# One encoder kernel: every fourth wide tile takes its products in mirrored order

## The chip, the cores and the metric

The kernel runs on one core of one Trainium2 chip. The metric is the device time of one execution in microseconds (us). Before the change three runs took 1983.12, 1983.80 and 1987.77 us, so the median is 1983.8 us.

## The reference

Two layers over 256 tokens of width 1024. Each layer is a normalisation, a projection to attention, Hyena and gate inputs, the two mixers, an output projection, and then a PEER block. The PEER block is what the change touches:

```
q = h @ wq                                   # 1024 -> 2048, per token
s = q . subkeys ; top 16 x top 16 -> 16 experts of 16384 per head
a = gelu(h . u_tab[expert])                  # first expert product
y = sum over heads and experts of g * a * v_tab[expert]
```

The kernel computes `h @ u` for all 16384 experts (128 tiles of 128 experts), multiplies the result by a routing weight that is zero for the experts not picked, and multiplies by `v` (128 more tiles).

## The kernel before, in words

All weights come from memory as one stream of tiles of 128 x 1024 numbers into a ring of four places. Every tile is split into a high part (ScalarE, L507, rounded to the short format that TensorE multiplies at full rate) and a low part, the rest (GpSimd or VectorE, L444). The activations are split the same way. A product is then high by high, high by low and low by high.

Two forms of this product stand in the kernel. In the trunk (`contract`, `product`; lines 1611 to 1635) each of the three products is a matmul of its own with 256 moving columns, one for each token. In the query projection (16 tiles a layer) and the first expert product (128 tiles a layer) `wide_tile` is used: the moving operand of the high weights is the high and the low activations side by side, so one matmul with 512 columns (L1646, the wide product) does two of the three, and one with 256 columns (L1648, the narrow product) does the third with the low weights. Both are added up in one bank of PSUM over eight steps k. Every matmul has its own weight load of 128 x 128, so that a tile is eight wide and eight narrow products and sixteen loads, always in the order wide, narrow, wide, narrow. The second expert product (`v_half`, L2045) has 512 columns in all three of its products.

The order of TensorE's queue is written out by hand. `wide_tile` waits for the low part of a half tile (`parts_ready`) before steps 0 and 4. A tile's last matmul raises `tile_done`. Behind that ScalarE copies the bank's right half out (L825, L849), splits the tile two ahead (L507), and GpSimd makes its low part (L444), which the tile two ahead waits for. VectorE adds the two halves and ScalarE applies the gelu, which frees the bank (`gelu_done`).

The wide tiles of a layer are called from five places: four query tiles in a row and then a loop with four a turn; `u_tile` for the first 60 expert tiles, four written out and the rest in loops with four a turn; `late_tile` for the last 68, with four in each of 16 turns of a loop, each turn begun by 32 small matmuls of routing weights (L1984), and two ahead of and two behind that loop.

Of the kernel before, what the change touches and what calls it, by code (L numbers as in the profile page):

```python
# [22 lines left out]
S = 256  # L23
# [16 lines left out]
KT = D // P  # L40
# [5 lines left out]
T_UP, T_OUT, T_WQ, T_U = 40, 48, 56, 72  # L46
# [3 lines left out]
AHEAD = 2  # L50
SORTED = 52
ROUTED = 60
# [45 lines left out]
def encoder_kernel(nc, x_in, stream, subkeys, cols, ffn_cols, w1_in, w2_in, w3_in, skip_in, rpb_in,  # L98
                   pos_in, dft_in, decay_in, spread_in, mask_in, mats_in, iota_in, out):
    ctx = ExitStack()  # L100
    with ctx:
        def sb(name, shape, dt=F32):
            return ctx.enter_context(nc.sbuf_tensor(name, shape, dt))
# [14 lines left out]
        w_hi = sb("w_hi", [P, 2 * AHEAD, HT], F32R)  # L118
        w_lo = sb("w_lo", [P, 2 * AHEAD, HT], F32R)
# [19 lines left out]
        bank = [ctx.enter_context(nc.psum_tensor(f"bank{i}", [P, 512], F32)) for i in range(8)]  # L139
# [24 lines left out]
        both_raw = raw_parts2[:, :, :].rearrange("p (b k) t -> p b k t", b=2)  # L164
        both_acts = act_parts[:, :, :, :]
# [1430 lines left out]
        def _(pe):  # L1596
            T = nc.tensor

            def pe_layer(l):
                def parts_ready(i, tile, half):  # L1600

                    pe.wait_ge(lo_ready[half].sem, lo_ready[half].at(l, i * RING + (tile + 1)))

                def weights(part_, tile, k):

                    return part_[:, 2 * (tile % AHEAD) + k // 4, (k % 4) * P:(k % 4 + 1) * P]

                def product(out_, tile, j, k, start, stop, parts=(act_hi, act_lo)):

                    hi, lo = parts  # L1610
                    T.matmul(out_, weights(w_hi, tile, j), hi[:, k, :], start=start, stop=False,
                             skip_group_check=True)
                    T.matmul(out_, weights(w_hi, tile, j), lo[:, k, :], start=False, stop=False,
                             skip_group_check=True)
                    return T.matmul(out_, weights(w_lo, tile, j), hi[:, k, :], start=False, stop=stop,
                                    skip_group_check=True)
# [19 lines left out]
                                       skip_group_check=True)  # L1636
                    return ins

                def wide_tile(out_, i, tile, both, wait=None):

                    for k in range(KT):
                        if k % 4 == 0:
                            parts_ready(i, tile, k // 4)
                        if wait is not None:
                            wait(k)
                        T.matmul(out_[:, 0:2 * S], weights(w_hi, tile, k), both[:, :, k, :],  # L1646
                                 start=(k == 0), stop=False, skip_group_check=True)
                        ins = T.matmul(out_[:, 0:S], weights(w_lo, tile, k), both[:, 0, k, :],  # L1648
                                       start=False, stop=(k == KT - 1), skip_group_check=True)
                    ins.then_inc(tile_done.sem, 1)  # L1650

                def trunk_part(n):
# [23 lines left out]
                def head_columns(i):  # L1676
                    return by_head[:, QUAD - 2 - 2 * i:2 * QUAD - 2 - 2 * i]
# [59 lines left out]
                for e in range(TT):  # L1737
                    ins = T.matmul(bank[5][e * FFN:(e + 1) * FFN, 0:P], w1[0:POS, :], pos[0:POS, e, :],
                                   start=True, stop=True)
                ins.then_inc(ffn_done.sem, 1)  # L1740

                for n in range(4):
                    if n == 1:
                        pe.wait_ge(tile_copied.sem, tile_copied.at(l, 8))
                        for i in range(2):
                            for j in range(4):
                                ins = T.matmul(bank[4][j * QUAD:(j + 1) * QUAD, 0:S], head_columns(i),
                                               qk_sq[:, 2 * j + i, :], start=(i == 0), stop=(i == 1))
# [3 lines left out]
                    for half in range(2):  # L1752
                        parts_ready(0, T_V + n, half)
                        k, part_ = 2 * n + half, 2 * (n % AHEAD) + half
                        for tt in range(TT):
                            tokens = slice(tt * P, (tt + 1) * P)
                            T.matmul(bank[6 + tt][:, :], raw_hi[1][:, k, tokens], w_hi[:, part_, :],
                                     start=(k == 0), stop=False)
                            T.matmul(bank[6 + tt][:, :], raw_hi[1][:, k, tokens], w_lo[:, part_, :],
                                     start=False, stop=False)  # L1760
                            ins = T.matmul(bank[6 + tt][:, :], raw_lo[1][:, k, tokens], w_hi[:, part_, :],
                                           start=False, stop=(k == KT - 1))
                    ins.then_inc(tile_done.sem, 1)
                    if n == 3:
                        pe.wait_ge(arg_ready.sem, arg_ready.at(l, 1))
                        pe.wait_ge(sin_done.sem, sin_done.at(l, 1))
                        for e in range(TT):
                            rows = slice(e * FFN, (e + 1) * FFN)
                            ins = T.matmul(bank[5][rows, 0:P], w2[rows, :], h1[rows, :], start=True, stop=True)
# [24 lines left out]
                for n in range(4):  # L1794
# [3 lines left out]
                    ins = T.matmul(bank[4 + n][:, :], dft[:, ri, e, 0:P], filters[:, ri, e, :], start=True, stop=True)  # L1798
# [35 lines left out]
                for h in range(NH):  # L1834
# [4 lines left out]
                    for qt in range(TT):  # L1839
                        for kt in range(TT):  # L1840
                            ins = T.transpose(bank[6][:, kt * S + qt * P:kt * S + (qt + 1) * P],
                                              probs[:, h % 2, qt, kt * P:(kt + 1) * P], identity)
# [15 lines left out]
                    for kt in range(TT):  # L1858
                        for j in range(2):
                            g = h - 1 + j  # L1860
                            ins = T.matmul(attn_ps[h // 2][j * HD:(j + 1) * HD, :], v_tok[:, kt, g * HD:(g + 1) * HD],
                                           probs_T[:, j, kt, :], start=(kt == 0), stop=(kt == TT - 1))
# [26 lines left out]
                for ct in range(4):  # L1889
                    for e in range(TT):  # L1890
                        for ri in range(2):
                            ins = T.matmul(bank[4 + ct][:, e * P:(e + 1) * P],
                                           spec_y[:, ri, e, ct * P:(ct + 1) * P], dft[:, 2 + ri, e, 0:P],
                                           start=(ri == 0), stop=(ri == 1))
# [4 lines left out]
                for k in range(4):  # L1899
                    pe.wait_ge(hyena_ready.sem, hyena_ready.at(l, k + 1))  # L1900
                    for j in (0, 1):
                        ins = product(bank[(8 + j) % 4][:, 0:S], T_UP + 4, 4 * j + k, 4 + k, k == 0, k == 3)
# [6 lines left out]
                def out_product(m, k):  # L1909

                    if k % 4 == 0:
                        parts_ready(0, T_OUT + m, k // 4)
                    if m == 0:
                        pe.wait_ge(up_used.sem, up_used.at(l, 8 + k + 1))
                    return product(bank[4 + m % 4][:, 0:S], T_OUT + m, k, k % 4, k == 0, k == KT - 1,
                                   (act_hi, act_lo) if k < 4 else (merged_hi, merged_lo))
# [16 lines left out]
                for m in range(8):  # L1933
# [5 lines left out]
                    for k in range(2 if m == 1 else 0, KT):  # L1939
# [3 lines left out]
                        ins = out_product(m, k)  # L1943
                    ins.then_inc(tile_done.sem, 1)

                for s in range(RING):
                    if s == 1:
                        mean_square(2)
                    wide_tile(bank[s % 4], 0, T_WQ + s, both_raw, trunk_part(2) if s == 0 else None)
                with pe.Fori(1, (T_U - T_WQ) // RING) as w:  # L1950
                    for s in range(RING):
                        pe.wait_ge(q2_ready.sem, q2_ready.at(l, w * RING + (s - 3)))
                        wide_tile(bank[s % 4], w, T_WQ + s, both_raw)
                pe.wait_ge(subk_in.sem, subk_in.at(l, 16))
                for n in range(8):
                    tt, g = n // 4, n % 4
# [4 lines left out]
                    for c in range(4):  # L1961
                        m = 4 * g + c
                        ins = T.matmul(bank[4 + g][:, c * P:(c + 1) * P], q2T[:, m, tt * P:(tt + 1) * P],
                                       subk[:, m, :], start=True, stop=True)
                    ins.then_inc(score_done.sem, 1)

                def u_tile(i, s, first):


                    if first + s >= 4:  # L1970
                        pe.wait_ge(gelu_done.sem, gelu_done.at(l, i * RING + (first + s - 3)))
                    wide_tile(bank[s % 4], i, T_U + first + s, both_acts)

                def late_tile(i, n):

                    pe.wait_ge(gelu_done.sem, gelu_done.at(l, i * RING + (ROUTED + n - (3 if n < AHEAD else 1))))
                    wide_tile(bank[n % 2], i, T_U + ROUTED + n, both_acts)

                def routing_weights(i, n):

# [21 lines left out]
                for s in range(RING):  # L2002
                    u_tile(0, s, 0)
                with pe.Fori(0, SORTED // RING - 1) as i:
                    for s in range(RING):
                        u_tile(i, s, RING)
                pe.wait_ge(slots_ready.sem, slots_ready.at(l, 1))
                for tt in range(TT):
                    for c in range(3):
                        ins = T.transpose(bank[6 + tt][:, c * P:(c + 1) * P], slots[:, tt, c, :], identity)  # L2010
                    ins.then_inc(slotT_done.sem, 1)
                with pe.Fori(0, (ROUTED - SORTED) // RING) as i:
                    for s in range(RING):
                        u_tile(i, s, SORTED)

                for n in range(AHEAD):
                    late_tile(0, n)
                pe.wait_ge(gelu_done.sem, gelu_done.at(l, ROUTED))
                with pe.Fori(0, TGROUPS // RING) as i:
                    for n in range(BURST):  # L2020
                        routing_weights(i, n)
                    for n in range(BURST):
                        late_tile(i, n + AHEAD)
                for n in range(LATE - AHEAD, LATE):
                    late_tile(0, n)
# [69 lines left out]
            for l in range(DEPTH):  # L2095
                pe_layer(l)
# [113 lines left out]
```

## Time and profile before

| | |
|---|---|
| median of three runs | 1983.8 us |
| the profiled execution | 1983.6 us |
| its span, first to last instruction | 1981.8 us |
| TensorE matmuls | busy 1975.0 us, 100% of the span, 11924 instructions |
| TensorE weight loads | busy 1717.0 us, 87% |
| GpSimd, VectorE, ScalarE | busy 81%, 63%, 56% |
| granted TensorE clock | 1.000 (2.4 GHz) |

A matmul's record is longer than its share of the engine: matmuls are pipelined, and a record runs from its start to a modelled end, so that records overlap. What one product costs is therefore read from the distance between two starts, not from its mean duration.

### The profile page before, as it was taken

To read this page: it belongs to the slowest core of one execution; us is meant where nothing else is said; L and a number is where in the kernel's file an instruction comes from. 1 tells how busy PE (TensorE), PEld (TensorE's weight loads), DVE (VectorE), ACT (ScalarE), POOL (GpSimd) and SP (SyncE) were. 2 spreads that over 40 slices of the span, in tenths; PEclk is the share of its full clock that TensorE was granted. 3 is DMA by queue.
4 is the path that set the end of the run, shared out by engine and by line. 5 is a ranking of instruction groups with operands and counts; after the bars stand their busy time and mean duration, and the time that the engine had idled before them with its cause. 6 is when DMAs were issued, how large, how long until landed. Compare 5 with 4: busy or idle time off the path is not lost.

```text
span 1981.8 us, 41411 instructions
## 1 busy us (share of the span) xinstructions
PE 1975.0 (100%) x11924; PEld 1717.0 (87%) x11924; DVE 1246.6 (63%) x2807; ACT 1119.1 (56%) x2455; POOL 1603.1 (81%) x1316
## 2 busy tenths in 40 slices
PE   9999999999999999999999999999999999999999
PEld 8999888888888888888888898888888888888887
DVE  6787589888886333333367865998888863333333
ACT  6565565655555555555575556666555555555554
POOL 7767979987778888888877678899877878888886
PEclk9999999999999999999999999999999999999999
DMA  9544645554445555555584446455544455555554
GB/s 279 171 140 150 210 160 182 189 178 160 160 159 167 193 191 192 195 194 190 196 234 163 138 159 211 161 190 184 174 163 165 159 169 194 191 191 193 194 195 149
DMA packets 103396, 358.41 MB, mean 181 GB/s; under 512 B 11744, under 2 KB 16802, under 8 KB 103076
## 3 DMA queue, kind: packets, MB, share of 16 engines
q1 hardware_dynamic: 102900, 355.41, 54.5%
q10 hardware_dynamic: 432, 2.18, 0.3%
q8 instruction: 36, 0.59, 0.1%
q14 instruction: 28, 0.23, 0.0%
HBM read 356.49 MB, written 1.05 MB: 180 GB/s over the span
## 4 chain that ended last, share of the span: by engine, by line
PE 60%; POOL 23%; issue 15%; POOLq 1%; DMA 0%; DVE 0%; SPq 0%; ACT 0%; DVEq 0%; ACTq 0%
PE bank L2045 35%; POOL w_lo L444 23%; PE bank L1646 14%; PE bank L1648 7%; PE bank L1984 3%; POOLq L442 0%; DMA ring<-stream 0%; POOLq L465 0%; PE bank L2071 0%; POOL e_lo L472 0%; SPq L409 0%; SPq L413 0%; DVE raw_lo L974 0%; PE bank L2010 0%; ACT w_hi L507 0%
## 5 line engine op out<-in xcount | busy, mean ns | idle before, releaser
L444 POOL TENSOR_TENSOR w_lo<-ring,w_hi 128x512 fp32r<-128x512 f32 x1048 | 1400.9, 1353 | 289.5 <-ACT w_hi L507 288.3
L507 ACT ACTIVATE w_hi<-ring 128x512 fp32r<-128x512 f32 x1312 | 753.3, 621 | 186.7 <-PE bank L1635 88.1
L1646 PE MATMUL bank<-act_parts,w_hi 128*128 128x512 f32 x2048 | 718.1, 396 | 0.2
L1648 PE MATMUL bank<-act_parts,w_lo 128*128 128x256 f32 x2048 | 569.6, 278 | 0.0
L444 DVE TENSOR_TENSOR w_lo<-ring,w_hi 128x512 fp32r<-128x512 f32 x256 | 236.7, 924 | 450.1 <-ACT w_hi L507 449.9
L1646 PEld LDWEIGHTS bank<-act_parts,w_hi 128*128 128x128 f32 x2048 | 384.1, 188 | 89.6 <-POOL w_lo L444 1.3
L2045 PE MATMUL bank<-w_hi,e_hi 128*128 128x512 f32 x1024 | 398.9, 390 | 0.2
L2045 PE MATMUL bank<-w_hi,e_lo 128*128 128x512 f32 x1024 | 398.4, 389 | 0.0
L2045 PE MATMUL bank<-w_lo,e_hi 128*128 128x512 f32 x1024 | 398.4, 389 | 0.0
L1648 PEld LDWEIGHTS bank<-act_parts,w_lo 128*128 128x128 f32 x2048 | 385.2, 188 | 0.0
L843 ACT ACTIVATE e_hi<-arena 128x256 fp32r (+1 forms) x256 | 106.8, 418 | 315.6 <-PE bank L2045 315.6
L472 POOL TENSOR_TENSOR e_lo<-arena,e_hi 128x256 fp32r<-128x256 f32 x256 | 191.7, 749 | 70.7 <-ACT e_hi L843 70.6
L2045 PEld LDWEIGHTS bank<-w_hi,e_hi 128*128 128x128 f32 x1024 | 192.2, 188 | 41.4 <-POOL e_lo L472 1.0
L2045 PEld LDWEIGHTS bank<-w_hi,e_lo 128*128 128x128 f32 x1024 | 192.2, 188 | 39.9
L2045 PEld LDWEIGHTS bank<-w_lo,e_hi 128*128 128x128 f32 x1024 | 192.2, 188 | 39.4
L849 ACT ACTIVATE norm_tmp<-bank 128x256 f32<-128x256 f32 x136 | 52.6, 387 | 202.9 <-PE bank L1648 202.9
L1630 PE MATMUL bank<-act_parts,w_hi 128*128 128x256 f32 x896 | 121.3, 288 | 0.0
L1630 PEld LDWEIGHTS bank<-act_parts,w_hi 128*128 128x128 f32 x896 | 111.2, 191 | 9.4 <-issue 7.9
L825 ACT ACTIVATE arena<-bank 128x256 f32<-128x256 f32 x120 | 46.1, 384 | 125.9 <-PE bank L1648 125.9
L1541 DVE TENSOR_TENSOR bank<-bank,norm_tmp 128x256 f32<-128x256 f32 x136 | 58.6, 431 | 63.2 <-ACT norm_tmp L849 63.2
L1523 DVE TENSOR_TENSOR weighted_j<-onehot_j,bank 128x512 f16<-128x512 f16 x256 | 95.2, 413 | 0.0
L1646 PE MATMUL bank<-raw_parts,w_hi 128*128 128x512 f32 x256 | 89.4, 394 | 0.0
(262 smaller groups left out, 2357.6 us busy)
## 6 DMA issues: line engine op xcount, KB each, us to landing
ring<-stream SPq DMA_DIRECT2D x654, 512.0 KB, 3.3
arena<-rpb_in SPq DMA_DIRECT2D x8, 512.0 KB, 8.5
arena<-dft_in SPq DMA_DIRECT2D x4, 512.0 KB, 5.8
arena<-subkeys ACTq DMA_DIRECT2D x2, 1024.0 KB, 6.8
ring<-stream SPq DMA_DIRECT2D x4, 256.0 KB, 4.6
xT<-x_in SPq DMA_DIRECT2D x4, 256.0 KB, 4.7
arena<-w_in SPq DMA_DIRECT2D x2, 512.0 KB
arena<-decay_in SPq DMA_DIRECT2D x2, 512.0 KB
```

The costliest lines, as they stand in the source:

```text
L444: eng.tensor_tensor(w_lo[:, part_, :], ring[:, tile % RING, half * HT:(half + 1) * HT], w_hi[:, part_, :].bitcast(F32), ALU.subtract).then ...
L472: pool.tensor_tensor(e_lo[:, n % AHEAD, :], experts[:, bass.ds(i * RING + n, 1), :].rearrange("p a t -> p (a t)"), e_hi[:, n % AHEAD, :].b ...
L507: nc.scalar.activation(w_hi[:, 2 * (tile % AHEAD) + half, :], ring[:, tile % RING, half * HT:(half + 1) * HT], ACT.Copy).then_inc(hi_ready ...
L843: nc.scalar.activation(e_hi[:, n % AHEAD, :], experts[:, bass.ds(i * RING + n, 1), :].rearrange("p a t -> p (a t)"), ACT.Copy).then_inc(e_ ...
L849: nc.scalar.activation(u_lo[:, n % 2, :], bank[n % 2][:, S:2 * S], ACT.Copy).then_inc(u_lo_ready.sem, 1)
L1523: ins = V.tensor_tensor(weighted_j[:, n % BURST, a, :, :, :], onehot_j[:, a, :, :].unsqueeze(1).to_broadcast(wide), pair_weights(a).unsque ...
L1541: V.tensor_tensor(u_ps, u_ps, u_lo[:, n % 2, :], ALU.add).then_inc(u_sum.sem, 1)
L1630: T.matmul(out_, weights(w_hi, tile, k), moving[:, k, :], start=(k == 0 and moving is hi), stop=False, skip_group_check=True)
L1646: T.matmul(out_[:, 0:2 * S], weights(w_hi, tile, k), both[:, :, k, :], start=(k == 0), stop=False, skip_group_check=True)
L1648: ins = T.matmul(out_[:, 0:S], weights(w_lo, tile, k), both[:, 0, k, :], start=False, stop=(k == KT - 1), skip_group_check=True)
L1984: ins = T.matmul(bank[ROUTE_BANKS[n]][:, t * NK:(t + 1) * NK], onehot_i[:, n % BURST, t // 2, :, t % 2], weighted_j[:, n % BURST, t // 2, ...
L2045: ins = T.matmul(bank[4 + 2 * half + tt][:, :], e_[:, n % AHEAD, tokens], w_[:, part_, :], start=first and w_ is w_hi and e_ is e_hi, stop ...
```

## The change

`wide_tile` gets a parameter `mirrored`. In a mirrored tile the steps with odd k take the narrow product first and the wide one behind it, so that the order of the tile is wide narrow, narrow wide, wide narrow, narrow wide, and so on. The products, their operands, their bank and the waits ahead of steps 0 and 4 are the same. It is switched on for one of four tiles: in the query loop for s == 0 (not for the first four tiles), in `u_tile` for s == 0 and in `late_tile` for n == AHEAD (2). The last matmul of a mirrored tile, which raises `tile_done`, is the wide product of step 7 where it was the narrow one.

```diff
-                def wide_tile(out_, i, tile, both, wait=None):
+                def wide_tile(out_, i, tile, both, wait=None, mirrored=False):
+                    def high(k, stop=False):
+                        return T.matmul(out_[:, 0:2 * S], weights(w_hi, tile, k), both[:, :, k, :],
+                                        start=(k == 0), stop=stop, skip_group_check=True)
+                    def low(k, stop=False):
+                        return T.matmul(out_[:, 0:S], weights(w_lo, tile, k), both[:, 0, k, :],
+                                        start=False, stop=stop, skip_group_check=True)
                     for k in range(KT):
...
-                        T.matmul(out_[:, 0:2 * S], weights(w_hi, tile, k), both[:, :, k, :],
-                                 start=(k == 0), stop=False, skip_group_check=True)
-                        ins = T.matmul(out_[:, 0:S], weights(w_lo, tile, k), both[:, 0, k, :],
-                                       start=False, stop=(k == KT - 1), skip_group_check=True)
+                        if mirrored and k % 2:
+                            low(k)
+                            ins = high(k, k == KT - 1)
+                        else:
+                            high(k)
+                            ins = low(k, k == KT - 1)
                     ins.then_inc(tile_done.sem, 1)
...
-                        wide_tile(bank[s % 4], w, T_WQ + s, both_raw)
+                        wide_tile(bank[s % 4], w, T_WQ + s, both_raw, mirrored=(s == 0))
...
-                    wide_tile(bank[s % 4], i, T_U + first + s, both_acts)
+                    wide_tile(bank[s % 4], i, T_U + first + s, both_acts, mirrored=(s == 0))
...
-                    wide_tile(bank[n % 2], i, T_U + ROUTED + n, both_acts)
+                    wide_tile(bank[n % 2], i, T_U + ROUTED + n, both_acts, mirrored=(n == AHEAD))
```

## Rows read from the trace of the kernel before

**Rows 1.** The page: busy time and share of the span, then the slices.
```profile
PE 1975.0 (100%) x11924; PEld 1717.0 (87%) x11924; DVE 1246.6 (63%) x2807; ACT 1119.1 (56%) x2455; POOL 1603.1 (81%) x1316
PEclk9999999999999999999999999999999999999999
```

**Rows 2.** TensorE's waits: who for whom, us in total, times, longest.
```profile
PE bank L2093 <- DVE w_rest L952: 1.1, 1, 1.1
PE bank L1611 <- DVE raw_lo L974: 0.9, 2, 0.6
```

**Rows 3.** The page's costliest groups: xcount | busy, mean ns | idle before.
```profile
L1646 PE MATMUL bank<-act_parts,w_hi 128*128 128x512 f32 x2048 | 718.1, 396 | 0.2
L1648 PE MATMUL bank<-act_parts,w_lo 128*128 128x256 f32 x2048 | 569.6, 278 | 0.0
L1646 PE MATMUL bank<-raw_parts,w_hi 128*128 128x512 f32 x256 | 89.4, 394 | 0.0
```

**Rows 4.** Line L1646 in three stretches: duration min/median/max, first and last start.
```profile
L1646 PE MATMUL bank<-raw_parts,w_hi x59: 391/391/391, 209.8 to 229.9; 128*128 128x512 f32 x59
L1646 PE MATMUL bank<-act_parts,w_hi x369: 395/398/403, 259.8 to 389.8; 128*128 128x512 f32 x185
L1646 PE MATMUL bank<-act_parts,w_hi x341: 392/392/395, 1241.8 to 1359.7; 128*128 128x512 f32 x171
```

**Rows 5.** Timeline from 500.38: start, us, engine, line, weight loads (PEld) too.
```profile
500.38 0.40 PE L1646 MATMUL bank<-act_parts,w_hi 128*128 128x512 f32 x1
500.38 0.19 PEld L1648 LDWEIGHTS bank<-act_parts,w_lo 128*128 128x128 f32 x1
...
500.61 0.28 PE L1648 MATMUL bank<-act_parts,w_lo 128*128 128x256 f32 x1
500.61 0.19 PEld L1646 LDWEIGHTS bank<-act_parts,w_hi 128*128 128x128 f32 x1
500.73 0.39 PE L1646 MATMUL bank<-act_parts,w_hi 128*128 128x512 f32 x1
...
505.23 0.40 PE L1646 MATMUL bank<-act_parts,w_hi 128*128 128x512 f32 x1
```

**Rows 6.** Timeline of TensorE, narrow products alone, then the next instruction.
```profile
113.22 1.12 PE L1635 MATMUL bank<-act_parts,w_lo 128*128 128x256 f32 x8
114.18 0.60 PE L1841 MATMUL bank<-mats,arena 128*128 128x128 f32 x4
114.54 2.16 PE L1630 MATMUL bank<-act_parts,w_hi 128*128 128x256 f32 x16
116.54 1.12 PE L1635 MATMUL bank<-act_parts,w_lo 128*128 128x256 f32 x8
```

**Rows 7.** Chain of waits, one merged piece of 512-column products: start, us.
```profile
643.43 342.83 PE bank L2045 x1512
```

**Rows 8.** Timeline of TensorE where wide tiles end and 512-column products begin.
```profile
643.15 0.28 PE L1648 MATMUL bank<-act_parts,w_lo 128*128 128x256 f32 x1
643.27 0.39 PE L2045 MATMUL bank<-w_hi,e_hi 128*128 128x512 f32 x1
643.50 0.39 PE L2045 MATMUL bank<-w_lo,e_hi 128*128 128x512 f32 x1
643.73 0.39 PE L2045 MATMUL bank<-w_hi,e_lo 128*128 128x512 f32 x1
643.96 0.40 PE L2045 MATMUL bank<-w_hi,e_hi 128*128 128x512 f32 x1
```

**Rows 9.** Timeline at a tile's end (1300.64, its last narrow product): all engines.
```profile
1299.16 2.56 POOL L444 TENSOR_TENSOR w_lo<-ring,w_hi 128x512 fp32r<-128x512 f32 x2 [0.22 <-ACT w_hi L507]
...
1300.64 0.28 PE L1648 MATMUL bank<-act_parts,w_lo 128*128 128x256 f32 x1
1300.76 0.39 PE L1646 MATMUL bank<-act_parts,w_hi 128*128 128x512 f32 x1
...
1300.96 0.39 ACT L825 ACTIVATE arena<-bank 128x256 f32<-128x256 f32 x1 [1.07 <-PE bank L1648]
...
1302.14 0.39 PE L1646 MATMUL bank<-act_parts,w_hi 128*128 128x512 f32 x1
```

**Rows 10.** Timeline of the weight loads: 64 loads of the subkey scores, merged.
```profile
246.40 7.37 PEld L1963 LDWEIGHTS bank<-arena 128*128 128x128 f32 x64
253.69 0.19 PEld L1646 LDWEIGHTS bank<-act_parts,w_hi 128*128 128x128 f32 x1
```

## The prediction

> **What bounds the kernel now.** I read the page's busy times first: matmuls cover 100% of the span, the clock is granted in full in every slice, and no other engine is above 81% [rows 1]. Next, who TensorE waited for: two entries, 2.0 us of 1981.8 [rows 2]. So the time is the number of products times the distance between their starts. Only something that changes this distance, or makes TensorE wait, can move the time. The reader is to see in the groups that the wide and the narrow products stand there with means of 396 and 278 ns and next to no idle time [rows 3]. These means can't be added: the records overlap. The distances have to come from starts.
>
> The third view is therefore one line over a long stretch. In the early expert tiles of layer 1 the wide products start at 1241.8 and, 340 pairs on, at 1359.7: 117.9 / 340 = 346.8 ns for a pair of one wide and one narrow product. In the query tiles of layer 0 it is 20.1 / 58 = 346.6 ns. In the early expert tiles of layer 0 it is 130.0 / 368 = 353.3 ns [rows 4]. The same code with the same operands thus runs in two rhythms, 6.5 ns a pair apart; I call the second the slow beat. In the late tiles it is (505.23 - 500.38) / 14 = 346.4 ns, and a pair is divided into about 230 ns from a wide start to the narrow one and 120 ns back (500.38, 500.61, 500.73) [rows 5].
>
> **What the change does to the distances.** A mirrored tile before had 8 steps from wide to narrow and 8 back, the last of them to the next tile's first product. Now it has 4 wide to narrow, 4 narrow to narrow, 4 narrow to wide, and 4 wide to wide, the last again over the tile's end (the next product is always another tile's wide one, for every mirrored place is followed by an unmirrored tile). I call the exchange of one pair (wide to narrow, narrow to wide) for one narrow to narrow plus one wide to wide a swap: 4 in a tile. Mirrored tiles in a layer: 3 in the query loop, 1 + 12 + 2 = 15 among the first 60 expert tiles, 16 in the late loop, together 34; with two layers 68 tiles and 272 swaps. No instruction, byte or wait is added.
>
> Narrow to narrow: the trunk's tiles have it, same shapes, also adding into one bank. Eight of them take 114.18 - 113.22 = 0.96 us, 120 ns each. With the high weights, 16 take 116.54 - 114.54 = 2.00 us, 125 ns, but that holds the start behind another kind of matmul [rows 6]. Wide to wide: the second expert product has 1512 in a row in 342.83 us, 226.7 ns each [rows 7]. Just behind a mixed stream the first three are 230 ns apart [rows 8]. So a swap's new half costs 120 + 227 = 347 ns where the old one cost 346.8, or 353.3 in the slow beat. I take 347: these are the longest undisturbed stretches of each neighbour. The nearest rows give the ends: low 345 (120 after the first product less the 2 ns by which 10 ns rows can err, plus 227), high 125 + 230 = 355. That is -2 to +8 ns a swap, -0.5 to +2.2 us in all.
>
> Why should it come out even? Each load begins with the start of the product ahead of it (500.38 and 500.61, both lines) [rows 5]: one load lies under one product, whichever kind follows. At 2.4 GHz 512 columns stream in 213.3 ns and 256 in 106.7. The pure streams show 226.7 and 120, that is 13.4 and 13.3 ns more each, independent of the width. In the mixed order the sum is the same, only divided otherwise (some 4 ns later for the narrow, 4 earlier for the wide start). A cost that each product brings along by itself doesn't depend on the order.
>
> The sum: of the 272 swaps 13 tiles x 4 = 52 lie in the slow-beat stretch (from 253.7 us [rows 10] to at least 389.8 [rows 4], 48 tiles of 2.83 us; I count 13 turns of four): 52 x (347 - 353.3) = -0.33 us. The other 220: 220 x (347 - 346.75) = +0.06 us. Together -0.3 us.
>
> The end of a tile: `tile_done` comes with the end of the last product's record. Before, the narrow product began about 116 ns ahead of the next tile and lasts 278. Now the wide one begins 227 ns ahead and lasts 396: 169 ns against 162 behind the tile's end, 7 ns later. Queued behind it are ScalarE's copy (1300.96), its splits, and GpSimd's low parts. What covers it: GpSimd's second half is ready at 1299.16 + 2.56 = 1301.72, and TensorE needs it at its fifth pair of the tile that begins at 1300.76, at 1302.14: 0.42 us to spare [rows 9]. The first half, taken as half of the two's 2.56 us, is ready at 1300.44 and needed at 1300.76: 0.32 us. Cost nothing; with the cover gone it would be 68 x 7 ns = 0.5 us.
>
> The waits at steps 0 and 4 stay in front of a wide product, since both k are even. Behind a mirrored tile the next first load may begin 227 ns ahead of its product and not 116, which asks for the wait to be over 0.11 us sooner. 0.3 us cover that too, and the load has a whole wide product to lie under, so being late by 0.1 us costs nothing either. DMAs and GpSimd's queue aren't moved.
>
> Own time of the profiled execution: span 1981.8 plus 1.8 around it = 1983.6. With -0.3: 1983.3. The median of the runs shown is 0.2 above this execution: 1983.5 us.
>
> **The rivals.**
>
> Slower, the slow beat spreads. The beat exists, holds for 130 us, and what starts or ends it no row tells. A mirrored tile shifts the phase at every second product. If that puts other stretches into the slow beat, each pair costs 6.5 ns more. Layer 1's early tiles alone (some 50 tiles, 400 pairs): +2.6 us, 1986.1. All 2304 - 400 = 1904 pairs: +12.4 us, 1995.9. It passes 0.3% (6.0 us) at 915 pairs. For it: two of the stretches that were measured differ for no reason in the code. One of the three runs before is 4 us above the others, about the price of it in one or two stretches. Against it: the late tiles are begun anew in each turn and show 346.4.
>
> Faster, the layer 0 beat breaks. The first expert tile is now a mirrored one, and a mirrored tile returns every four. If the beat doesn't survive, 400 pairs win 6.5 ns: -2.6 us, 1981.2. This is within 0.3%.
>
> Faster, like neighbours lose the 13 ns. If the extra belonged to the change of width, a swap would win 2 x 13.35 ns: 272 x 26.7 = 7.3 us, 1976.5. Against it speak the pure streams themselves, which have it [rows 6, 7]; for it only that no row shows two wide in a row on a moving operand made of two pieces. The Trainium skill, TensorE: Matmul & The Clock Gate, section Back-to-back issue gap, has columns / 2.4 + 2.5 ns for a product with nothing else; by this estimate a pair is 325 ns, and a swap that reached it would save 22 ns, 6 us in all. The trace doesn't agree with it for this stream: 347.
>
> Slower by a little, two narrow ones can't hide their loads. The 64 loads of the subkey scores come (253.69 - 246.40) / 64 = 114 ns apart, under products of half the width [rows 10]: a load needs about as long as a narrow product streams (106.7), so nothing is left over, and a wide product's slack could now be out of reach. Price: 125 for 120 and 230 for 227, +8 ns a swap, +2.2 us: 1985.7. The same page, section LDWEIGHTS (loading the stationary operand), gives 128 / 1.2 = 107 ns, where the records say 0.19 us [rows 5]; by 107 this rival would cost nothing, by 188 narrow products could not be 120 apart at all.
>
> **How the numbers follow.** The sum holds (within 1 us of 1983.5): 0.48. The beat of layer 0 breaks: 0.21. The narrow loads show: 0.10. The slow beat spreads: 0.13, of which 0.08 over 915 pairs. The 13 ns vanish: 0.08. A difference of 0.3% or 6 us is about what a measurement of this kernel tells from none; faster by more 0.08, slower by more 0.08, within 0.84. The range: down to the broken beat with 0.5 us to spare, 1980.7; up past one more stretch in the slow beat and the narrow loads together (1983.5 + 2.6 + 2.2 = 1988.3), 1988.0. It leaves out the vanished 13 ns and most of the wide spread, under 2 in 10.
>
> **What the profile after would show.** In a mirrored tile the starts should be about 231, 120, 116, 227 ns apart, and two pairs 694 together. If the narrow to narrow distance is over 125 or the wide to wide over 231, the term of the swap is wrong. The wide products' first and last starts over layer 1's early stretch should give 346.8 ns; 353 would be the spread beat, and 347 in layer 0 the broken one. TensorE's waits should still be two entries. What would make the forecast wrong as a whole: a distance that depends on the neighbour by more than 20 ns, or a new wait of TensorE for the low parts.

## The result, and the profile after

The changed kernel takes 1993.3 us (median of 6 runs, 1992.5 to 1993.9) where the kernel before takes 1983.5 (6 runs, 1981.9 to 1987.8). The ratio is 1.0043, 95% interval 1.0031 to 1.0054: slower by 0.4%, where the forecast was 1983.5 us with a range of 1980.7 to 1988.0. The profiled execution spans 1990.7 us against 1981.8.

TensorE is still busy all the time at the full clock, and its waits are again two short ones. The first fence is from the page, the second lists for whom TensorE waited (us in total, times, longest); they answer to [rows 1, 2].

```profile
PE 1984.4 (100%) x11924; PEld 1722.1 (87%) x11924; DVE 1245.9 (63%) x2807; ACT 1117.8 (56%) x2455; POOL 1600.2 (80%) x1316
PEclk9999999999999999999999999999999999999999
```
```profile
PE bank L2103 <- DVE w_rest L952: 1.1, 1, 1.1
PE bank L1681 <- DVE norm_tmp L1100: 0.5, 1, 0.5
```

So no wait came in; the products stand further apart. The wide products (L1642 is the wide one now) in the early expert tiles of the two layers, to be held against [rows 4] (duration min/median/max, first and last start):

```profile
L1642 PE MATMUL bank<-act_parts,w_hi x328: 392/398/404, 259.9 to 375.0; 128*128 128x512 f32 x164
L1642 PE MATMUL bank<-act_parts,w_hi x325: 392/398/403, 1246.0 to 1360.0; 128*128 128x512 f32 x163
```

That is 115.1 / 327 = 352.0 ns a pair in layer 0 and 114.0 / 324 = 351.9 in layer 1. Before it was 353.3 and 346.8. In the late loop the chain of waits shows the routing matmuls that begin a turn; here are the first, the second and the last that it names in layer 0 (start, us):

```profile
430.45 1.85 PE bank L1994 x32
443.60 1.85 PE bank L1994 x32
...
628.12 1.85 PE bank L1994 x32
```

(628.12 - 430.45) / 15 = 13.178 us a turn. The same view of the kernel before, second and last turn of layer 0:

```profile
442.79 1.85 PE bank L1984 x32
...
624.88 1.85 PE bank L1984 x32
```

(624.88 - 442.79) / 14 = 13.006 us a turn.

The timeline of TensorE through a mirrored tile of layer 0 (start, us, count). Two products of one kind in a row are merged. The tile's end is inside the last row with x2, and unmirrored tiles follow:

```profile
299.95 0.40 PE L1646 MATMUL bank<-act_parts,w_lo 128*128 128x256 f32 x2
300.18 0.63 PE L1642 MATMUL bank<-act_parts,w_hi 128*128 128x512 f32 x2
300.65 0.39 PE L1646 MATMUL bank<-act_parts,w_lo 128*128 128x256 f32 x2
300.88 0.62 PE L1642 MATMUL bank<-act_parts,w_hi 128*128 128x512 f32 x2
301.35 0.40 PE L1646 MATMUL bank<-act_parts,w_lo 128*128 128x256 f32 x2
301.58 0.63 PE L1642 MATMUL bank<-act_parts,w_hi 128*128 128x512 f32 x2
302.05 0.39 PE L1646 MATMUL bank<-act_parts,w_lo 128*128 128x256 f32 x2
302.27 0.63 PE L1642 MATMUL bank<-act_parts,w_hi 128*128 128x512 f32 x2
302.74 0.28 PE L1646 MATMUL bank<-act_parts,w_lo 128*128 128x256 f32 x1
302.85 0.40 PE L1642 MATMUL bank<-act_parts,w_hi 128*128 128x512 f32 x1
303.08 0.28 PE L1646 MATMUL bank<-act_parts,w_lo 128*128 128x256 f32 x1
303.20 0.40 PE L1642 MATMUL bank<-act_parts,w_hi 128*128 128x512 f32 x1
303.44 0.28 PE L1646 MATMUL bank<-act_parts,w_lo 128*128 128x256 f32 x1
303.56 0.40 PE L1642 MATMUL bank<-act_parts,w_hi 128*128 128x512 f32 x1
303.80 0.28 PE L1646 MATMUL bank<-act_parts,w_lo 128*128 128x256 f32 x1
303.91 0.40 PE L1642 MATMUL bank<-act_parts,w_hi 128*128 128x512 f32 x1
```

In the mirrored tile two pairs take (302.27 - 300.18) / 3 = 0.697 us, 348.3 ns a pair. The mirrored order by itself is thus between the two beats. In the unmirrored tile behind it three pairs take 303.91 - 302.85 = 1.06 us, 353.3 ns each, the slow beat. To see all the tiles behind mirrored ones, I took the distance from each wide tile's first start to the next one's, in ns, from the same traces:

```
early loop, layer 1, four tiles a turn (mirrored one first in the changed kernel)
before     2773 2774 2773 2773 | 2774 2773 2773 2774
changed    2792 2814 2830 2831 | 2791 2814 2830 2831
late loop, second and third tile of a turn:  before 2773 2773   changed 2814 2830
```

2773 is eight pairs of 346.7; a stream in the slow beat has 2830, 2831 and 2819 in turn, on average eight of 353.3. The mirrored tile costs 19 ns, the three unmirrored ones behind it 41, 57 and 57. Not every turn is like that: in each layer one turn of the early loop has its three unmirrored tiles in the fast beat (2774, 2773, 2773 in layer 0). Added up by stretch, after minus before:

| stretch | layer 0 | layer 1 |
|---|---|---|
| query tiles | +0.5 us | +0.5 us |
| first 60 expert tiles | -0.3 | +2.3 |
| two tiles ahead of the late loop | +0.1 | +0.1 |
| late loop | +2.75 | +2.75 |
| two tiles behind it | +0.1 | +0.1 |

Together 8.9 us, all of the span's 8.9. By kind of tile, the 220 unmirrored ones take 8.3 us more than before and the 68 mirrored ones 0.8 us more (1.1 more outside layer 0's early tiles, 0.4 less in them, most of which were in the slow beat before); the routing matmuls take 0.2 less. So nearly all of the loss is the slow beat in unmirrored tiles. It was not drawn by chance: all six runs lie within 1.4 us of each other, and the same distances come back in nearly every turn of both layers.

### The profile page after: what moved, and what is told of

It is laid out like the page before. It is cut to its first block, busy times and chain, and to the rows that moved or that the text cites. A ratio compares the mean times of both kernels' runs of the same rounds, so it can differ in the third digit from the quotient of the medians.

```text
span 1990.7 us, 41411 instructions
## 1 busy us (share of the span) xinstructions
PE 1984.4 (100%) x11924; PEld 1722.1 (87%) x11924; DVE 1245.9 (63%) x2807; ACT 1117.8 (56%) x2455; POOL 1600.2 (80%) x1316
## 4 chain that ended last, share of the span: by engine, by line
PE 60%; POOL 23%; issue 15%; POOLq 1%; DMA 0%; DVE 0%; SPq 0%; ACT 0%; DVEq 0%; ACTq 0%
PE bank L2055 35%; POOL w_lo L444 23%; PE bank L1642 15%; PE bank L1646 7%; PE bank L1994 3%; POOLq L442 0%; DMA ring<-stream 0%; POOLq L465 0%; PE bank L2081 0%; POOL e_lo L472 0%; SPq L409 0%; SPq L413 0%; DVE raw_lo L974 0%; PE bank L2020 0%; ACT w_hi L507 0%
## 5 line engine op out<-in xcount | busy, mean ns | idle before, releaser
L1642 PE MATMUL bank<-act_parts,w_hi 128*128 128x512 f32 x2048 | 708.7, 399 | 0.2
L1646 PE MATMUL bank<-act_parts,w_lo 128*128 128x256 f32 x2048 | 533.6, 280 | 0.0
L1642 PEld LDWEIGHTS bank<-act_parts,w_hi 128*128 128x128 f32 x2048 | 367.5, 188 | 71.6 <-POOL w_lo L444 1.3
L1646 PEld LDWEIGHTS bank<-act_parts,w_lo 128*128 128x128 f32 x2048 | 386.3, 189 | 22.1
L849 ACT ACTIVATE norm_tmp<-bank 128x256 f32<-128x256 f32 x136 | 52.3, 385 | 210.0 <-PE bank L1646 114.0
L1630 PEld LDWEIGHTS bank<-act_parts,w_hi 128*128 128x128 f32 x896 | 111.2, 191 | 9.4 <-issue 7.9
L1642 PE MATMUL bank<-raw_parts,w_hi 128*128 128x512 f32 x256 | 88.8, 399 | 0.0
```

The source lines that it names most:

```text
L849: nc.scalar.activation(u_lo[:, n % 2, :], bank[n % 2][:, S:2 * S], ACT.Copy).then_inc(u_lo_ready.sem, 1)
L1630: T.matmul(out_, weights(w_hi, tile, k), moving[:, k, :], start=(k == 0 and moving is hi), stop=False, skip_group_check=True)
L1642: return T.matmul(out_[:, 0:2 * S], weights(w_hi, tile, k), both[:, :, k, :], start=(k == 0), stop=stop, skip_group_check=True)
L1646: return T.matmul(out_[:, 0:S], weights(w_lo, tile, k), both[:, 0, k, :], start=False, stop=stop, skip_group_check=True)
```

## Experiments

Theory A: a mirrored tile leaves the stream behind it in the slow beat. Theory B: each mirrored tile simply has a price. All edits below are to the changed kernel, unless it says otherwise. Where a batch of runs had the kernel before beside it, its runs spread by 6 to 13 us, from 1981 or 1982; the second profile of the kernel before, near the end, says why. Little is therefore read from the medians alone, and most from turns and pairs in the profiles.

**Mirrored only in the late loop, first tile of a turn.**

```diff
-  wide_tile(bank[s % 4], w, T_WQ + s, both_raw, mirrored=(s == 0))
+  wide_tile(bank[s % 4], w, T_WQ + s, both_raw)
-  wide_tile(bank[s % 4], i, T_U + first + s, both_acts, mirrored=(s == 0))
+  wide_tile(bank[s % 4], i, T_U + first + s, both_acts)
```


> Mirrored only in the late loop's first tile of a turn (n == 2); query tiles and the first 60 expert tiles as before. Theory A (a mirrored tile leaves the tiles behind it, up to TensorE's next change of work, in the slow beat of 353.3 ns a pair): a turn takes 13.18 us as in the changed kernel, where it took 13.007 before; 32 turns x 0.171 = +5.5 us. Layer 1's early stretch back at 346.8 ns a pair. Theory B (each mirrored tile has a price of its own, 9 us / 68 = 0.13 us): 32 x 0.13 = +4.3 us.

Measured: 1989.2 us (1986.8 to 1994.1), 1.0022 of before (1.0011 to 1.0033). Chain of waits, late loop of layer 0:

```profile
431.50 1.85 PE bank L1994 x32
...
629.21 1.85 PE bank L1994 x32
```

(629.21 - 431.50) / 15 = 13.18 us a turn, as A said. Not as A said: in this profile the early stretches, with no mirrored tile at all, are in the slow beat in both layers (2830 a tile), and so are the query tiles. The profiled execution is the slowest of its nine, 1994 us; two early stretches at 2.6 us each would account for its distance to the median.

**The same, last tile of a turn.**

```diff
-  wide_tile(bank[n % 2], i, T_U + ROUTED + n, both_acts, mirrored=(n == AHEAD))
+  wide_tile(bank[n % 2], i, T_U + ROUTED + n, both_acts, mirrored=(n == AHEAD + BURST - 1))
```


> As the run before this one, but the mirrored tile is the last of the turn (n == 5), with the routing matmuls right behind it. Theory A: no wide tile stands behind it, so only the mirrored tile's own swaps are paid (2 to 4 ns each): turn 13.02 us, in all +0.5 us. Theory B: the same price as in first place, +4.3 us.

Measured: 1984.4 us (1984.0 to 1988.8), ratio 1.0008 (0.9998 to 1.0018).

```profile
441.14 1.85 PE bank L1994 x32
...
623.32 1.85 PE bank L1994 x32
```

(623.32 - 441.14) / 14 = 13.013 us a turn in the very same number of mirrored tiles. B is out: four swaps cost 6 ns here, and 171 where three unmirrored tiles stand behind them.

**All wide tiles mirrored.**

```diff
-  ..., mirrored=(s == 0))        # and (n == AHEAD)
+  ..., mirrored=True)            # the first four query tiles too
```


> All 288 wide tiles mirrored. Theory A: no tile is left that could run in the slow beat; a mirrored tile takes 348.6 ns a pair (read in the changed kernel), so against before 15 ns more a tile, and 4.7 ns a pair less in layer 0's early stretch: +2 to +3 us, 1986. Theory B: 288 x 0.13 us = +38 us.

Measured: 1984.55 us, ratio 0.9993 (0.9984 to 1.0003). Ten of the eleven runs lie within 1 us (1984.07 to 1984.96). The profile fell on the eleventh, in which the granted clock was 0.56 in every stretch (mean 0.556) and the span 3272.4 us, so the same kernel was run again:

> All wide tiles mirrored, once more, for a profile at the full clock. Theory A: 348.5 to 349 ns a pair in every stretch of both layers, no 353.3 and no 346.7 anywhere; a turn 13.03 to 13.10 us; the time 1984.5 us with all runs within 1 us, where those of the kernel before spread over 10 us.

Measured: 1984.6 us, ratio 0.9995 (0.998 to 1.001), eight of ten runs from 1984.2 to 1985.0, the others 1986.3 and 1988.8. Early stretches of both layers:

```profile
L1642 PE MATMUL bank<-act_parts,w_hi x332: 390/396/398, 259.7 to 374.9; 128*128 128x512 f32 x166
L1642 PE MATMUL bank<-act_parts,w_hi x328: 390/396/398, 1245.9 to 1359.7; 128*128 128x512 f32 x164
```

115.2 / 331 = 348.0 and 113.8 / 327 = 348.0 ns a pair, the same in both; whole tiles, 2787 or 2786 ns apart, give 348.4, for in this order the first and the last start don't lie at the same place. Turns are 13.047 us. Four times as many mirrored tiles as in the change cost 1.0 us in the sum by stretch, where the change cost 8.9. B is out again.

**One mirrored tile a layer.**

```diff
-  wide_tile(bank[s % 4], i, T_U + first + s, both_acts, mirrored=(s == 0))
+  wide_tile(bank[s % 4], i, T_U + first + s, both_acts, mirrored=(first == 0 and s == 0))
```
with the query and late tiles unmirrored.

> One mirrored tile a layer, the first expert tile; all others as before. Theory A: it alone puts layer 1's early stretch (400 pairs) into the slow beat, 353.3 ns a pair there: +2.6 us; layer 0's was slow before and stays so. Theory B: 2 x 0.13 = +0.3 us, and layer 1 keeps 346.8 ns.

Measured: 1991.0 us (1990.0 to 1994.4), ratio 1.0033 (1.0020 to 1.0045), more than either theory. Layer 1's early stretch, and the late loop of layer 0, in which nothing is mirrored, then that of layer 1:

```profile
L1642 PE MATMUL bank<-act_parts,w_hi x324: 393/398/404, 1245.7 to 1359.7; 128*128 128x512 f32 x162
```
```profile
430.72 1.85 PE bank L1994 x32
...
628.92 1.85 PE bank L1994 x32
```
```profile
1419.80 1.85 PE bank L1994 x32
...
1614.90 1.85 PE bank L1994 x32
```

114.0 / 323 = 352.9: in both layers the mirrored tile is followed by 48 in the slow beat. The profile alone doesn't prove that the tile did it: six profiles here have early stretches that begin without a mirrored tile, and 6 of these 12 stretches begin slow too. For it speak the 2814, 2830 and 2831 ns of the three tiles behind it, the same as behind nearly every mirrored tile of the changed kernel, and the times: none of the nine runs is below 1990.0 us, where half of those of the kernel before beside it are below 1984.7. The late loops took 13.21 and 195.10 / 15 = 13.01 us a turn with the same instructions. So a stretch can also be slow, turn after turn over 32 foreign matmuls each, without any mirrored tile: the 13.21 are +3.3 us for 16 turns.

What the loop makes of a slow stream seems to depend on where its pattern of 2830, 2831 and 2819 ns is cut. Where the last whole tile distance ahead of the routing matmuls was 2819 or 2820, the unmirrored tiles behind them were fast (three entries: both layers of the run with the last tile of a turn mirrored, and layer 0 of the second profile of the kernel before). Where it was 2831, at the entry of this slow loop, and 2830, in each of its turns, the next turn was slow.

**One swap instead of four, late loop alone.**

```diff
-  if mirrored and k % 2:
+  if mirrored and k == 1:
```


> Mirrored tile in the late loop alone (n == 2), and in it only step 1 narrow first: one swap a turn where the run with all odd steps had four. Theory A (a swap throws the stream off its phase, and it falls into the slow beat for the rest of the turn): a turn 13.16 to 13.20 us, +5 us or more in all. Theory C (a cost for each swap, 0.17 us / 4 in a turn): 13.05 us, +1.4 us.

Measured: 1983.9 us (1981.6 to 1988.3), ratio 0.9994 (0.9977 to 1.0011). A failed: the first turn, entered from a slow stream, is slow in both layers, the unmirrored tiles of all fifteen behind it are fast (2773), 13.01 us a turn.

**How many swaps, and where.** Four kernels with the change's 34 tiles a layer, differing in the line above: `k == 1`; `k in (1, 3)`; `k in (1, 3, 5)`; `k == 7`.

> The changed kernel's 34 tiles a layer, but narrow first in step 1 alone: one swap a tile. Theory D (a swap only shifts the phase of the stream; one swap leaves a stream in the beat that it was in, four end in the slow one): +5 to +12 ns a swap, 68 swaps, under 1 us; the time is that of the kernel before plus that, 1982 to 1990 by the beats it enters, with 2773 and 2830 ns tiles both to be found. Theory A (any swap ends in the slow beat): 2814 to 2830 ns in the three tiles behind each, 1993.

> The same with two swaps a tile (steps 1 and 3). Theory D: if it needs a certain length of the mirrored order, 2 of 4 steps are the first that could tell: either fast tiles behind it (1983) or slow ones (1992). A cost of the swaps alone: half of the four-swap tile's 18.6 ns, 9 ns x 68 = 0.6 us.

> Three swaps a tile (steps 1, 3, 5), so that the tile ends wide, narrow like an unmirrored one. If the swap over the tile's end, in front of the next tile's first product, is what throws the next tile into the slow beat, the tiles behind are fast here: 1983. If the length of the mirrored order does it: slow, 1992.

> One swap a tile, in step 7, over the tile's end: its wide product stands next to the following tile's first. If the tile's end matters: slow tiles behind, 1992. If only the number of swaps: as with step 1, 1982 to 1990.

| narrow first in | median us (range, runs) | ratio, 95% | late turn behind the first | unmirrored early tiles, ns |
|---|---|---|---|---|
| step 1 | 1988.3 (1988.1 to 1988.9, 10) | 1.0015 (1.0006 to 1.0025) | 13.01 us | 2819 to 2831 but for two fast turns in layer 0 |
| 1, 3 | 1995.6 (1994.2 to 1996.7, 4) | 1.0049 (1.0032 to 1.0066) | 13.19 | 2819 to 2831 |
| 1, 3, 5 | 1993.8 (1993.3 to 1996.2, 4) | 1.0045 (1.0029 to 1.0062) | 13.18 | 2819 to 2832 |
| 7 | 1988.2 (1987.3 to 1989.9, 10) | 1.0016 (1.0007 to 1.0026) | 13.02 | 2814 to 2831 but for one to three fast turns a layer |

One swap a turn is enough to bring the early streams into the slow beat and to keep them there in most turns, at the tile's start or over its end; three without one over the tile's end do it too. So neither a swap over the tile's end nor a certain length of the mirrored order is needed. In the late loop, where routing matmuls stand ahead of each turn, one swap ends fast and two or more slow. Theory D, that one swap leaves a stream in its beat, held for no early stretch as a whole.

**Larger groups.** All tiles, no mirroring; eight wide then eight narrow, and four and four:

```diff
-  if mirrored and k % 2:
-      low(k)
-      ins = high(k, k == KT - 1)
-  else:
-      high(k)
-      ins = low(k, k == KT - 1)
+  high(k)
+  if k % 8 == 7:                       # k % 4 == 3 in the second
+      for j in range(k - 7, k + 1):    # k - 3
+          ins = low(j, j == KT - 1)
```


> In all wide tiles the eight wide products first, then the eight narrow ones. Theory A (two beats belong to the strict change of wide and narrow): no beat, wide 226.7 and narrow 120 ns as in the pure streams, 346.7 ns a pair in every stretch; 1981 to 1982 us, and runs within 1 us. Theory C (like neighbours cost 3.6 ns a swap, as read in the mirrored tiles): 7 swaps a tile x 288 x 3.6 ns = +7.3 us on 1981, 1988.

> Four wide, four narrow, twice a tile, in all wide tiles. Theory A: between the mirrored order (348.6 ns a pair) and the pure streams (346.7): 347 to 348, 1981.5 to 1983 us, little spread. Theory C: 6 swaps a tile, +6.2 us on 1981, 1987.

Measured: 2005.3 us (4 runs; ratio 1.0094, 1.0058 to 1.0129) and 1990.0 us (10 runs; 1.0019, 1.0006 to 1.0032). Both expectations of A failed, and both times are also above C's, 1988 and 1987. For eight, what ended the idle time of the weight loads (PEld) of wide products from 1246 to 1360 us (us, times):

```profile
  POOL w_lo L444: 7.9, 30
```

The wait ahead of step 4 for the low part of the second half now comes after four wide products (0.92 us) instead of four pairs (1.39 us), and the 0.42 us to spare of [rows 9] are gone. A tile that waits takes some 2940 to 2990 ns, one that doesn't some 2800. For four this wait stands where it stood, TensorE and its loads have no such wait, and yet:

```profile
L1642 PE MATMUL bank<-act_parts,w_hi x327: 387/396/398, 1245.7 to 1359.8; 128*128 128x512 f32 x164
```

The tiles are 2807 or 2806 ns apart, 350.8 ns a pair, in both layers: 34 ns a tile over the fast beat for six swaps, 5.6 each, where C had 3.6. The runs lie within 1.2 us of each other. The starts in this trace, in ns after each product of a group of eight, beside those of the other orders:

```
four and four    wide 233 236 228 233   narrow 117 120 117 117
                 wide 235 233 236 224   narrow 118 120 120 120
mirrored         236 116 113 232 231 113 119 234      (wide, narrow, narrow, wide, ...)
fast beat        232 118 231 112 233 117  or  230 117
slow beat        233 117 241 120 236 113
```

Wide products behind narrow ones are 228 to 236 ns apart here, 233.6 on average, not the 226.7 of [rows 7].

**A foreign matmul, nothing mirrored.** To the kernel before, at the end of each turn of the early loop:

```diff
+  pe.wait_ge(score_copied.sem, score_copied.at(l, 8))
+  T.matmul(bank[6][:, 0:P], w_rest[:, :], w_rest[:, :], start=True, stop=True)
```


> The kernel before, no tile mirrored, with one small foreign matmul (128 columns) behind every fourth tile of the early loop, so 12 a layer. Theory E (any disturbance that comes again and again moves a stream into the slow beat, in which it then stays): 2830 ns for the undisturbed tiles of the loop in both layers after a few turns, +2 us beside the matmuls' own 24 x 0.2 us. Theory F (only like neighbours do): the undisturbed tiles keep the beat they entered with, 2773 in at least one layer.

Measured: 1989.9 us, ratio 1.0028 (1.0018 to 1.0038). The undisturbed tiles of four successive turns in layer 0 (second tile of each) are 2830, 2819, 2773, 2831 ns, and so on in the same rotation; in layer 1 the same. Three turns of four slow, every fourth fast: E for the most part, F not at all. Both early stretches were slow already ahead of the first foreign matmul, so it is the rotation that tells: the foreign matmul brings the stream out of the slow beat and, a turn later, into it again. So the mirrored order isn't needed for it, a disturbance of another kind does it too, and where that leaves the stream seems to have a rule, since it repeats with a period of four turns.

**The kernel before, unchanged, a second profile.**

> The kernel before, unchanged, for a second profile. If the beat of a stretch is drawn anew in each execution: at least one of its four long stretches (early and late, two layers) shows another beat than in the first profile (slow, fast, fast, fast), or the runs' times spread by 5 us or more in steps of 2.6 and 3.3 us. If the beat belongs to the program: the same beats and the same time within 1 us.

Measured: 1984.1 us (1981.6 to 1989.5), ratio 1.000 (0.999 to 1.001). The two early stretches, then the late loop of layer 0:

```profile
L1646 PE MATMUL bank<-act_parts,w_hi x333: 392/392/395, 259.8 to 374.8; 128*128 128x512 f32 x167
L1646 PE MATMUL bank<-act_parts,w_hi x324: 395/398/403, 1245.7 to 1359.8; 128*128 128x512 f32 x162
```
```profile
441.18 1.85 PE bank L1984 x32
...
623.27 1.85 PE bank L1984 x32
```

115.0 / 332 = 346.4 in layer 0, 114.1 / 323 = 353.3 in layer 1; the first profile had it the other way round [rows 4]. The turn is 182.09 / 14 = 13.006 us. The beat is drawn anew in each execution, stretch by stretch; the two late loops were fast in both profiles. The prices found (2.6 us for an early stretch, 3.3 for a late one) are enough for the spread of this kernel's runs: with all four slow they add up to 11.8 us. That the runs differ by nothing else is not shown.

**A version of both findings.** Query and early tiles all mirrored, in the late loop only the last tile of a turn:

> All query tiles and the first 60 expert tiles mirrored, in the late loop only the last tile of a turn. If both findings add up: 348.5 ns a pair early, turns of 13.013 us, in all 1981 + 0.2 + 1056 pairs x 1.7 ns = 1983.0 us, with little spread; that is below the median of the kernel before (about 1984.8) by 0.1%. If the late loop's fast entry hung on what ran before it, turns of 13.2 us in one or both layers: +3.3 us each.

Measured: 1983.5 us (1982.9 to 1984.5, 11 runs) beside 1984.5 for the kernel before (1981.4 to 1988.7, 25 runs); ratio 0.9997 (0.9988 to 1.0006). Turns of 13.01 us and 348.4 ns a pair came in both layers as expected. It beats the changed kernel; against the kernel before it makes no difference that was measured, but its runs spread over 1.6 us instead of 7.3.

## Why the prediction was wrong

- What bounds the kernel (TensorE's starts, no waits): right, before and after.
- The swap, forecast at 347 ns for the old 346.8, bounds -2 to +8: the bounds held, the value was low. A mirrored tile costs 19 ns for four swaps, so +4.7 each. Mirrored tiles outside layer 0's early stretch took 1.1 us more, where the sum had +0.06; those in it took 0.4 less, where it had -0.33. The term that was priced came out right by offsetting errors: in the mirrored tiles of the changed kernel two wide products in a row are 233 ns apart on average (over the 231 that the forecast had named as a sign against this term) and two narrow ones 114.6, together 347.5, where the pure streams gave 227 and 120. What was missed are the neighbours left unlike, taken at their old price: wide to narrow is 234.5 and narrow to wide 115.8 in such a tile, 350.4 for the 346.7 of before.
- The end of a tile, the waits at steps 0 and 4, GpSimd's lead: right, nothing was late.
- **The step that failed** is the one under the sum that left each stretch in the beat that [rows 4] show. It took the slow beat for a property of one stretch. It is a state that any stretch can be in, and a disturbance each turn brings the stream into it. This cost 8.3 us, where the sum had nothing. The rival that said so was the outcome, with a chance of 0.13. Its size, 6.5 ns a pair, was right; it reached most of the 1760 pairs (2 x 110 x 8) of unmirrored tiles, of which some 300 in layer 0 were slow before.
- The rival in which the beat of layer 0 breaks, 0.21, got the sign wrong: a repeated disturbance feeds the slow beat. The vanished 13 ns and a narrow load that shows (a distance over 125 ns between narrow products) were not seen. The two signs that were to make the forecast wrong as a whole, a distance off by more than 20 ns and a new wait for the low parts, didn't come either; the one that came was the wide products' distance in layer 1, 351.9 ns for 346.8, which had been named for the spread of the beat.
- The evidence was there. Two stretches of the same code differed by 6.5 ns a pair, and three runs spread by 4.7 us in a kernel without waits. The forecast named both as support of the rival and then weighed them lightly, against a single group of late tiles.

What stays open: what the beat is in the chip. The runs show two fast patterns and one slow one, that a stream without disturbance nearly always stays in its own (one execution passed from 2773 to 2830 in the middle of an early stretch without any edit there), and that where a disturbance leaves it depends on what was before. They don't show which resource it waits for in the 6.5 ns. The rival that other engines' traffic sets the beat had no experiment of its own. The traces speak against it: from 1250 to 1355 us the kernel before ran fast in one profile and slow in the other, with GpSimd busy 96.5 and 94.7 us, VectorE 98.6 and 97.0, and the DMA engines 57% and 56%, and the pattern of three pairs doesn't follow their work, which comes by the tile.

## What to carry to other kernels

When TensorE never waits, read the distances between starts in every stretch of the same code, and in more than one execution: if they differ, a stream can have more than one rhythm, and the spread of the runs may be made of it. Such a rhythm is a state to be kept, so an edit of the order is judged by what it does to the tiles behind it, not only by its own products. A few edited tiles in a uniform stream can cost more than all of them edited, and pure streams don't price a mixed one: here they gave each of the two new distances wrong by 5 to 6 ns, and said nothing on the old ones beside them.

## What the runs showed of the hardware that was not expected

- A strict change of 512- and 256-column products runs at 346.7 or at 353.3 ns a pair at the same full clock, by execution. The slow one repeats every three pairs (1060 ns).
- All tiles mirrored is slower than the fast beat and faster than the slow one, 348.4 ns a pair, and 18 of its 21 runs lie within 1 us (1984.07 to 1984.96).
- One execution of eleven of that kernel had a granted clock of 0.56 in every stretch of its 3272.4 us, neither 0.5 nor 1 (1.2 and 2.4 GHz), with TensorE busy throughout; its pairs took 576 ns. What brought it about isn't known.
